# A hybrid S5 and attention trunk on one core: chunk order in the first column group of the two-phase FFN layers, and the last residuals of the attention layer

## What is computed

```python
def rmsnorm(x, g):
    xf = x.astype(jnp.float32)
    y = xf * lax.rsqrt(jnp.mean(xf * xf, axis=-1, keepdims=True) + EPS)
    return (y * g.astype(jnp.float32)).astype(x.dtype)

def swiglu(x, w1, w3, w2):
    return (jax.nn.silu(x @ w1) * (x @ w3)) @ w2
...
    for i in range(DEPTH):
        h = h + 0.5 * swiglu(rmsnorm(h, ffn1_norm[i]), ffn1_w1[i], ffn1_w3[i], ffn1_w2[i])
        hn = rmsnorm(h, mix_norm[i])
...
            m = stick_breaking_mixer(hn, sb_w_qkv[j], sb_w_o[j])
        h = h + m
        h = h + 0.5 * swiglu(rmsnorm(h, ffn2_norm[i]), ffn2_w1[i], ffn2_w3[i], ffn2_w2[i])
        gate = jax.nn.sigmoid(rmsnorm(h, ple_norm[i]) @ ple_gate[i])
        h = h + (p[i].astype(h.dtype) @ ple_proj[i]) * gate
```

## Time and profile before

| | us |
|---|---|
| median of 3 runs | 1102.69 |
| lowest and highest run | 1099.95, 1102.89 |
| the profiled execution's own time | 1098.89 |
| its span, first to last instruction | 1096.9 |
| TensorE matmuls busy | 1066.8 |
| VectorE busy | 774.2 |
| ScalarE busy | 588.1 |
| GpSimd busy | 277.1 |

### The profile page before, as it was taken

The page is one execution under the profiler, slowest core; times in us unless marked ns, Lnnn a source line. Parts: engine busy times, 40 slices in busy tenths (PEclk is TensorE's granted clock), DMA queues, the critical chain, the costliest instruction groups (busy, mean ns, idle before and its releaser), DMA issues.

```text
span 1096.9 us, 18767 instructions
## 1 busy us (share of the span) xinstructions
PE 1066.8 (97%) x7606; PEld 979.2 (89%) x7606; DVE 774.2 (71%) x893; ACT 588.1 (54%) x796; POOL 277.1 (25%) x279
## 2 busy tenths in 40 slices
PE   6899999989999999999999999999999999999997
PEld 6899999979999888888998888888999888888896
DVE  6788766888757777766687776666555667676666
ACT  6644436642236555554565555454677655554543
POOL 8799998961002000000220000011011200000021
PEclk9999999999999999999999999999999999999999
DMA  8565655432146566666655666656533456666552
GB/s 215 154 191 173 190 173 154 141 110 78 40 135 194 161 198 187 193 191 189 194 175 175 190 192 192 185 184 198 170 118 115 137 173 191 194 183 197 187 183 76
DMA packets 179674, 183.07 MB, mean 167 GB/s; under 512 B 16128, under 2 KB 173456, under 8 KB 179600
## 3 DMA queue, kind: packets, MB, share of 16 engines
q1 hardware_dynamic: 179456, 181.99, 55.2%
q10 hardware_dynamic: 144, 0.04, 0.0%
HBM read 180.95 MB, written 1.05 MB: 166 GB/s over the span
## 4 chain that ended last, share of the span: by engine, by line
PE 72%; DVE 6%; issue 1%; ACT 1%; POOL 0%; POOLq 0%; DVEq 0%; ACTq 0%
PE acc L1804 32%; PE acc L1806 17%; PE bank L1468 3%; PE bank L1469 2%; PE bank L1470 2%; DVE w_lo L987 2%; PE acc L1468 2%; PE acc L1470 2%; PE acc L1469 2%; DVE op_both L1000 1%; PE acc L1600 1%; PE acc L1694 1%; PE bank L1637 1%; PE stat L1624 1%; PE misc L1600 0%
## 5 line engine op out<-in xcount | busy, mean ns | idle before, releaser
L987 DVE TENSOR_TENSOR w_lo<-raw,w_hi 128x1024 fp32r<-128x1024 f32 x346 | 449.1, 1308 | 207.5 <-ACT w_hi L646 206.6
L646 ACT ACTIVATE w_hi<-raw 128x1024 fp32r<-128x1024 f32 x346 | 356.5, 1040 | 239.5 <-PE acc L1806 89.5
L1804 PE MATMUL acc<-op_both,w_hi 128*128 128x512 f32 x1056 | 368.7, 393 | 2.1 <-DVE op_both L1000 1.6
L1806 PE MATMUL acc<-op_both,w_lo 128*128 128x256 f32 x1056 | 295.7, 280 | 0.0
L1804 PEld LDWEIGHTS acc<-op_both,w_hi 128*128 128x128 f32 x1056 | 197.6, 187 | 47.1 <-DVE op_both L1000 2.4
L1806 PEld LDWEIGHTS acc<-op_both,w_lo 128*128 128x128 f32 x1056 | 199.6, 189 | 0.0
L1804 PE MATMUL acc<-g_all,w_hi 128*128 128x512 f32 x528 | 183.2, 392 | 0.0
L1468 PE MATMUL bank<-op_both,w_hi 128*128 128x256 f32 x576 | 168.5, 293 | 7.0 <-DVE op_both L1000 4.1
L1469 PE MATMUL bank<-op_both,w_lo 128*128 128x256 f32 x576 | 163.1, 283 | 0.0
L1470 PE MATMUL bank<-op_both,w_hi 128*128 128x256 f32 x576 | 163.0, 283 | 0.0
L466 POOL TENSOR_TENSOR square_sum<-squares 128x512 f32<-128x512 f32 x9 | 12.9, 1436 | 583.6 <-issue 579.6
(11 more groups left out here) (319 smaller groups left out, 1636.1 us busy)
## 6 DMA issues: line engine op xcount, KB each, us to landing
raw<-in_ffn_w_dram SPq DMA_DIRECT2D x258, 512.0 KB, 4.0
raw<-in_sb_w_qkv_dram SPq DMA_DIRECT2D x24, 512.0 KB, 3.6
raw<-in_s_w_glu_dram SPq DMA_DIRECT2D x16, 512.0 KB, 3.4
raw<-in_ple_gate_dram SPq DMA_DIRECT2D x16, 512.0 KB, 3.4
raw<-in_s_w_in_dram SPq DMA_DIRECT2D x8, 512.0 KB, 3.5
raw<-in_sb_w_o_dram SPq DMA_DIRECT2D x8, 512.0 KB, 3.4
raw<-in_ffn_w_dram SPq DMA_DIRECT2D x12, 256.0 KB, 3.3
raw<-in_ple_proj_dram SPq DMA_DIRECT2D x4, 512.0 KB, 3.6
```

The costliest lines, as they stand in the source:

```text
L646: act.activation(w_hi[:, slot, 0:width], raw[:, slot, 0:width], ACT.Copy).then_inc(hi_done, 1)
L987: dve.tensor_tensor(w_lo[:, slot, 0:width], raw[:, slot, 0:width], w_hi[:, slot, 0:width].bitcast(F32), ALU.subtract).then_inc(lo_done, 1)
L1804: pe.matmul(pairs[h][:, m].rearrange("p i t -> p (i t)"), wh, x.rearrange("p i t -> p (i t)"), start=first, stop=False, skip_group_check=True)
L1806: return pe.matmul(pairs[h][:, m, 0, :], wl, x[:, 0, :], start=False, stop=last, skip_group_check=True)
```

## The change

Four edits. In group 0 of each two-phase layer the second and third chunk change places: the order is now w1 upper, w3 upper, w1 lower, w3 lower, in the load queue, on TensorE and in the banks. `stat_sum` keeps its place in the group's third chunk, `stat_spread` in the fourth; the wait for `x_new` and the gates now stands before the second chunk, `turn_p` before the third. The first copy of the low half and `sum_a` wait for the third chunk instead of the second, in group 0 alone. In the attention layer, the rounded and low drop of head 14 go ahead of softplus and `drop_of` of head 15. At its end, VectorE takes the last two residuals one behind the other, then chunk n0+33, both operands, and chunk n0+34; ScalarE makes the last operand ahead of chunk n0+34.

```diff
--- before.py
+++ after.py
@@ -376,7 +376,11 @@
             def load_ffn_in_two(st):
                 w1, w3, w2 = (w[st.layer] for w in ffn_weights[st.kind])
                 n = st.n0
-                for g in range(NG):
+                for half in range(2):
+                    for w in (w1, w3):
+                        load(n, n % RING, a_chunk(w, half, slice(0, 256)), True)
+                        n += 1
+                for g in range(1, NG):
                     for w in (w1, w3):
                         load_group(n, w, 256 * g)
                         n += 2
@@ -734,7 +738,7 @@
                 for g in range(NG):
                     n = n0 + 4 * g
                     split(n + 3)
-                    copy_low(0, n + 2)
+                    copy_low(0, n + 2 if g else n + 3)
                     if g == 0:
                         split(n + 4)
                         split(n + 5)
@@ -940,17 +944,22 @@
                     else:
                         if s > 1:
                             weights_of(s - 2)
+                        if s == NH - 1:
+                            rounded_drop(s - 1)
                         if s < NH:
                             softplus_part(s)
-                            rounded_drop(s - 1)
+                            if s < NH - 1:
+                                rounded_drop(s - 1)
                             split(n0 + 14 + s)
                         if s >= 3:
                             j = (s - 3) // 2
                             act.wait_ge(o_done, 2 * j + 2)
                             act.activation(op_hi[:, HALF[o_set], j, :], o_bank, ACT.Copy).then_inc(op_hi_done, 1)
-                for j in range(NB):
+                for j in range(NB - 1):
                     split(n0 + 31 + j)
                     prep(nxt.v, nxt.u, [j])
+                prep(nxt.v, nxt.u, [NB - 1])
+                split(n0 + 34)
 
             act.preload_act_table_set("exp_and_others")
             split(0)
@@ -1151,7 +1160,7 @@
                 copied = (2 * NG + NB) * (st.f - 1)
 
                 def sum_a(g):
-                    dve.wait_ge(pe_done, n0 + 4 * g + 2)
+                    dve.wait_ge(pe_done, n0 + 4 * g + (2 if g else 3))
                     dve.wait_ge(low_copied, copied + 2 * g + 1)
                     dve.wait_ge(silu_done, base + g)
                     dve.tensor_tensor(a_n[:, :, :], pairs[0][:, :, 0, :], low_part[:, 0], ALU.add).then_inc(a_taken, 1)
@@ -1417,20 +1426,30 @@
                         if s < NH:
                             drop_of(s)
                     else:
+                        if s == NH - 1:
+                            low_drop(s - 1)
                         if s < NH:
                             drop_of(s)
-                            low_drop(s - 1)
+                            if s < NH - 1:
+                                low_drop(s - 1)
                             split(n0 + 14 + s)
                         if s >= 3:
                             j = (s - 3) // 2
                             dve.wait_ge(op_hi_done, KD * o_set + j + 1)
                             dve.tensor_tensor(op_lo[:, HALF[o_set], j, :], o_bank, op_hi[:, HALF[o_set], j, :].bitcast(F32),
                                               ALU.subtract).then_inc(op_lo_done, 1)
-                for j in range(NB):
+                for j in range(2):
                     dve.wait_ge(pe_done, n0 + 29 + j)
                     take_out(j)
                     split(n0 + 31 + j)
                     op_low(nxt.v, nxt.u, j)
+                for j in range(2, NB):
+                    dve.wait_ge(pe_done, n0 + 29 + j)
+                    take_out(j)
+                split(n0 + 33)
+                op_low(nxt.v, nxt.u, 2)
+                op_low(nxt.v, nxt.u, 3)
+                split(n0 + 34)
 
 
             for b in range(NB):
@@ -1829,18 +1848,20 @@
                     n = n0 + 4 * g
                     if g:
                         pe.wait_ge(a_taken, base + g)
-                    for half in range(2):
-                        up(n + half, 0, half, ready=g > 0)
                     if g == 0:
+                        up(n, 0, 0, ready=False)
                         pe.wait_ge(x_new, 4 * v + 4)
                         pe.wait_ge(gate_ready, st.e)
                         if st.q:
                             pe.wait_ge(gate_taken, 4 * st.q)
+                        up(n + 1, 1, 0)
                         if nxt.kind == "ple":
                             turn_p(nxt.q)
-                        up(n + 2, 1, 0, hooks={2: lambda: stat_sum(v)})
+                        up(n + 2, 0, 1, ready=False, hooks={6: lambda: stat_sum(v)})
                         up(n + 3, 1, 1, hooks={6: lambda: stat_spread(v)})
                     else:
+                        for half in range(2):
+                            up(n + half, 0, half)
                         pe.wait_ge(b_taken, base + g)
                         for half in range(2):
                             up(n + 2 + half, 1, half)
```

## The result

The changed kernel took 1112.73 us (median of 6 runs, 1108.11 to 1115.3), the kernel before 1102.79 us beside it (6 runs, 1099.95 to 1103.49). The ratio is 1.0094, with a 95% interval of 1.0076 to 1.0112: slower by 9.9 us (8.4 to 12.4). The direction was forecast, the size was not: 1112.73 lies above the range, which ended at 1111.5. The profiled execution took 1115.3 us, the highest of the six, over a span of 1113.3.

A forecast was written before the change was run, and what follows sets the result against it. TensorE's matmuls fill 97% of the span, so a new gap there is paid in full. Layers A, B and C sum to 2.85 + 2.0 + 0.9 = 5.75, say +5.7 us: forecast 1108.4 us, range 1103.5 to 1111.5.

The forecast's parts named there:

- The chain and the stall: Two-phase layers, group 0: low part, mean and diagonals queue behind the later copy, stalling TensorE's spread 2.1 us per layer.
- c + 3.70: When VectorE starts the diagonals, counted from c, the moment ScalarE starts the group's first low-part copy.
- about c + 4.0: When TensorE's spread can start, in us after ScalarE starts the first low-part copy.
- A: Layer A, ffn2 of layer 0: forecast +2.85 us, from a 2.1 stall and 0.75 for the factors.
- The factors: VectorE's row copy of factors, 1.4 us after the spread, comes 0.75 later: paid in layers A and C, hidden in B.
- Layer B: ffn1 of layer 1: operand wait goes, new residual wait of 0.4, gain 0.1; spread stalls 2.1, factors hidden; +2.0 us.
- The attention: Last head pair before layer C: TensorE no longer waits for the rounded drop, gain 0.8 us.
- Layer C: ffn2 of layer 1 with the attention before it: -0.8 - 1.4 + 0.3 + 2.1 + 0.75, forecast +0.9 us.
- term (c): Start of layer C: VectorE work ahead of chunk 2, slowed beside GpSimd's sums; 0.3 us taken, 1.6 late if all slowed.
- if a wait for chunk 2's low part in C passed 1 us: Stated sign that the forecast would be wrong, at the start of layer C.
- The clock falls: Rival: each new TensorE stall costs a return to 1.2 GHz, 1.4 us of work lost, forecast 1112.6; chance 0.02.
- On that base the forecast is 1108.4: Forecast moved from the profiled execution (1098.89 us, giving 1104.6) to the median of runs, 3.8 above it.

The follow-up runs named there:

- experiment 1: The changed kernel, with the next group's first chunk, the mean and the diagonals taken ahead of the late copy and its sum; 1101.75 us against 1104.66, ratio 0.9979.
- experiment 2: The kernel before, with only the first copy of the low half in group 0 waiting one chunk longer; 1114.13 us against 1104.66, ratio 1.0082.
- experiment 3: The kernel before, with only the change's edits in the attention layer; 1104.31 us against 1104.66, ratio 0.9991.
- experiment 7: The kernel of experiment 1 without the edits in the attention layer; 1103.95 us against 1102.29 for the kernel before, ratio 1.0019.
- experiment 5: The changed kernel with the repair of experiment 1 in layer B (ffn1 of layer 1) only; 1109.5 us against 1102.29, ratio 1.0064.
- experiment 11: The kernel of experiment 1 with chunk n0+34's rounding and low part ahead of the last operand pair, measured again; 1101.14 us against 1101.89, ratio 0.9998.

## Why the prediction was right in kind and wrong in size

- **The chain and the stall: right.** "c + 3.70", "about c + 4.0" and "a stall of 2.1 us" in all three layers were measured as 3.70 and 4.04 in A, and the stall as 2.0 us three times; counted from chunk 3's first matmul to chunk 4's, 2.2. Experiments 1 and 2 show that the late copy with its queue is the cause.
- **The factors: mis-sized.** 0.75 was taken in A and C. The row copy came 1.19 behind the spread, not 1.4, and chunk 4 to chunk 6 grew by 0.45 in both. The forecast for A was 2.85, measured 2.65.
- **Layer B: right but for the clock.** The wait for the residual came (0.27, 0.4 at the chunk's start), the operand wait went. With the stall of layer A, B would be 2.0, as forecast; measured 3.8, in all three traces that have the stall there. No trace shows the stall in B without a fall, so the 2.0 is inferred.
- **The attention: right.** "Gain 0.8": the stretch got shorter by 0.9 (experiments 1 and 3, absent in 7).
- **Layer C, term (c): mis-sized.** "I take 0.3", with a far bound of 1.6. Chunk 2's low part was late by 1.4, near that bound, and so of the 1.4 of the operand wait only 0.1 was won. The text gave this as a sign that it would be wrong: "if a wait for chunk 2's low part in C passed 1 us". It was 1.13. I had reasoned that one low part and one pair had lost time beside two sums; here three `op_low` lost some 2.5 us beside the two sums and the addition behind them, and no low part lost any. Even the 1.53 that the rows gave would have made 0.6 (872.6 + 1.53 against 873.5), not 0.3. Layer C and attention came to 1.65 against +0.9.
- **The clock: the step that failed.** "The clock falls" had a chance of 0.02, by one gap of 2.7 us in one execution with no fall behind it. That row was read rightly, but it doesn't carry over to the new stalls: behind stalls of only 2.0 us a fall came in 6 of 11. The rival's price was nearly right: it said 1.4 us each, and they cost 1.8 in B, 0.6 to 0.7 in A and 0.4 in C by chunk 8. The runs without a trace bear the falls out. The mean granted clock was 0.9907 over the six runs of the change, 0.9918 and 0.9905 over the four each of experiments 2 and 5, and 0.9934 to 0.9944 over the 6 to 29 runs of every kernel without these stalls, the kernel before of the three later sessions included. One fall of 3.4 us at 1.2 GHz takes 0.0015 from such a mean, so the change had, as an estimate, some two falls a run. The Trainium skill (TensorE: Matmul & The Clock Gate, section "Why this matters for your kernels") warns of idle gaps between matmul bursts, longer ones than these; here 2.0 us was enough in 6 of 11, and the measurement decides.
- **The sum.** Forecast 5.7. The traced parts without a fall would be 2.65 + 2.0 + 1.65 = 6.3, well within the range. With the falls they come to 8.1 (in B) and 8.8 (in A and B), and the measured 9.9 has an interval from 8.4 to 12.4: 8.1 is just outside of it, 8.8 inside. Of the 4.2 missed, 1.8 to 2.5 are the clock and 1.1 is term (c), less 0.6 for the factors in A and C; the other 1.1 to 1.8 no trace accounts for.
- **The base.** "On that base the forecast is 1108.4": this held, since the medians compare like with like. But the profiled execution of before was a lucky one, with three fast phases and no fall of the clock behind that gap, and that of after the slowest of its six; of the 16.4 us between the two spans 2.6 lie ahead of any edit and 5.7 are the pace, neither of them shown to be the change.

## What to carry to other kernels

Moving one wait later on an in-order engine moves all that is queued behind it there; look for the instruction behind it that is wanted first (here two small diagonals), and move that ahead together with what it stands on. A stall of 2 us on a TensorE that is never idle may cost its clock as well: price it, as here in layer B, at up to twice its length where nothing downstream has slack, and less where a wait follows that can take up the slower matmuls. Before you read anything from the difference of two traces, compare two traces of the same kernel.

## What was not expected of the hardware

- **The clock behind short stalls.** In 6 of 11 stalls of 2.0 us at the spread the granted clock went to 0.50 (1.2 GHz) for some 3 to 4 us behind them: 3 of 3 in B, 2 of 4 in A, 1 of 4 in C. Ahead of each, TensorE had been busy since the layer's start but for waits of at most 1.1 us. At the layer starts of the other kernels, with no wait there over 1.2 us, no trace shows a fall. In the stretch from 216 to 240 us, which no edit touches, TensorE's longer waits are 1.1 to 2.3 us each, and 4 of 14 traces show a fall there, one of them (experiment 7, at 229.6 us) behind waits of 1.1 and 1.4 us. The length of a single gap doesn't decide by itself, since 2.7 us passed twice without a fall; what does decide stays open.
- **Two paces.** A pair of fp32 matmuls with 512 and 256 columns took 0.3467 or 0.3533 us for a whole first phase of 100 us, at a granted clock of 1.00. 26 of 42 first phases in 14 traces were slow (8 of 14 in A, 12 in B, 6 in C); the second phases were always at 0.3467. The two traces of the kernel before had 1 of 6 slow, the two of the change 5 of 6, too few to say whether an edit shifts the odds; experiment 11's kernel, with the same order of chunks and slow in all three in its trace, was no slower than before by its median. It makes 1.9 us a phase, so up to 5.7 us of difference between executions, more than most of the edits here are worth. No experiment was aimed at its cause, and it stays open.
- **VectorE behind GpSimd.** The four `op_low` took 4.25 us (4.23 in experiment 1) where two pairs elsewhere take 0.88 each, and a low part took 1.72 instead of 1.22. The loss is a wait, not a slower rate. In layer C of the change three of the four ended 0.28 us behind the GpSimd instruction beside them: at 883.90, 885.35 and 886.23, where the sums and the addition ended at 883.62, 885.07 and 885.95. In the 14 traces all 169 `op_low` over 0.6 us ended 0.28 or 0.29 us behind a GpSimd instruction, and all 843 low parts over 1.3 us ended 1.07 to 1.09 behind one; the 492 `op_low` with no GpSimd instruction beside them took 0.47 to 0.49. So term (c) is better added up from when each sum ends than from a factor of slowing. No run moved or removed the sums themselves.
